# Ones times ones on TensorE: 253 matmuls into unread PSUM banks, in the waits of a decoder step on one Trainium2 core

## The reference

```python
x = x + 0.5 * _swiglu(_rmsnorm(x, lw['g_ffn1']), lw['w1_gate'], lw['w1_up'], lw['w1_down'])
h = _rmsnorm(x, lw['g_mix'])
proj = h @ lw['w_in']
...
y_a = _rmsnorm(attend(q_a, k_a, v_a, logf_a), lw['g_out_a'])
...
h_m, C, n, m = _mlstm(q_m, k_m, v_m, i_pre, log_f_m, C0, n0, m0)
y_m = jax.nn.sigmoid(o_m).reshape(B, T, H_M, HEAD_DIM) * _rmsnorm(h_m, lw['g_out_m']).astype(x.dtype)
y = jnp.concatenate([y_a.reshape(B, T, W_A), y_m.reshape(B, T, W_M)], axis=-1) @ lw['w_out']
x = x + y
x = x + 0.5 * _swiglu(_rmsnorm(x, lw['g_ffn2']), lw['w2_gate'], lw['w2_up'], lw['w2_down'])
```

## Time and profile before

| | |
|---|---|
| median of 3 runs | 2433.18 us (2431.02 to 2445.05) |
| profiled execution | 2432.46 us, span 2430.5 us |
| TensorE matmul busy | 2353.8 us, 97% of the span, 17537 instructions |
| TensorE weight load busy | 2279.3 us, 94% |
| VectorE busy | 1245.9 us, 51% |
| ScalarE busy | 842.9 us, 35% |
| chain that ended last, by engine | TensorE 92%, VectorE 5%, ScalarE 1%, DMA 1% |
| mean granted TensorE clock | 0.979 |

### The profile page before, as it was taken

How to read it: one execution, slowest core, us unless ns; L and a number is a source line. 1 busy time by engine, 2 the same in 40 slices (tenths; PEclk the granted TensorE clock), 3 DMA queues, 4 the chain that set the end, 5 groups by cost and what they waited for, 6 DMA issues and landing times.

```text
span 2430.5 us, 47588 instructions
## 1 busy us (share of the span) xinstructions
PE 2353.8 (97%) x17537; PEld 2279.3 (94%) x17537; DVE 1245.9 (51%) x1848; ACT 842.9 (35%) x1109; POOL 83.6 (3%) x96
## 2 busy tenths in 40 slices
PE   7999999999999999997999898999999999999998
PEld 6999999999999999875999667999999999999998
DVE  6554444454454464563457665464445444455543
ACT  4433333333332443341234232443333233333332
POOL 2000000000000010000001240000000000000000
PEclk9999999999999999987999897999999999999999
DMA  5555555555554444454545332455555445555553
GB/s 159 179 158 170 166 162 173 171 162 168 165 163 167 153 158 148 151 175 152 168 160 172 97 107 70 164 165 167 162 166 162 166 169 167 170 158 167 161 170 127
DMA packets 175660, 383.90 MB, mean 158 GB/s; under 512 B 18949, under 2 KB 44669, under 8 KB 175245
## 3 DMA queue, kind: packets, MB, share of 16 engines
q1 hardware_dynamic: 172736, 375.98, 48.9%
q0 software_dynamic: 2432, 5.57, 0.7%
q10 hardware_dynamic: 416, 1.32, 0.2%
HBM read 373.09 MB, written 9.70 MB: 157 GB/s over the span
## 4 chain that ended last, share of the span: by engine, by line
PE 92%; DVE 5%; ACT 1%; issue 1%; DMA 1%; POOL 0%; SPq 0%; ACTq 0%; DVEq 0%; POOLq 0%
PE ps L1487 29%; PE ps L1489 28%; PE ps L1488 28%; DVE w_lo L882 1%; PE ps L1713 1%; PE ps L1572 1%; PE ps L1890 1%; PE ps L1535 1%; PE ps L1726 0%; PE ps L1881 0%; PE ps L1542 0%; ACT w_hi L568 0%; DMA x_rows<-in_x_sample 0%; DVE xt L908 0%; POOL C L521 0%
## 5 line engine op out<-in xcount | busy, mean ns | idle before, releaser
L882 DVE TENSOR_TENSOR w_lo<-w_raw,w_hi 128x1024 fp32r<-128x1024 f32 (+1 forms) x690 | 788.8, 1185 | 1034.9 <-ACT w_hi L568 1034.3
L568 ACT CAST w_hi<-w_raw 128x1024 fp32r<-128x1024 f32 (+1 forms) x690 | 669.2, 1017 | 1322.1 <-PE ps L1489 1319.3
L1487 PE MATMUL ps<-x_hi,w_hi 128*128 128x288 f32 (+1 forms) x2752 | 815.9, 296 | 5.2 <-DVE w_lo L882 3.2
L1489 PE MATMUL ps<-x_hi,w_lo 128*128 128x288 f32 (+1 forms) x2752 | 813.4, 296 | 0.0
L1488 PE MATMUL ps<-x_lo,w_hi 128*128 128x288 f32 (+1 forms) x2752 | 808.1, 294 | 0.0
L1487 PEld LDWEIGHTS ps<-x_hi,w_hi 128*128 128x128 f32 x2752 | 517.3, 188 | 6.4 <-DVE w_lo L882 3.3
L1488 PEld LDWEIGHTS ps<-x_lo,w_hi 128*128 128x128 f32 x2752 | 521.5, 189 | 0.1
L1489 PEld LDWEIGHTS ps<-x_hi,w_lo 128*128 128x128 f32 x2752 | 517.8, 188 | 0.0
L1487 PE MATMUL ps<-hid_hi,w_hi 128*128 (+1 forms) x1376 | 407.2, 296 | 1.5 <-DVE X L1053 1.5
L1488 PE MATMUL ps<-hid_lo,w_hi 128*128 (+1 forms) x1376 | 406.9, 296 | 0.0
L1489 PE MATMUL ps<-hid_hi,w_lo 128*128 (+1 forms) x1376 | 406.8, 296 | 0.0
(11 more groups left out here) (405 smaller groups left out, 1465.4 us busy)
## 6 DMA issues: line engine op xcount, KB each, us to landing
w_raw<-in_w_down SPq DMA_DIRECT2D x178, 512.0 KB
w_raw<-in_w_gate SPq DMA_DIRECT2D x320, 256.0 KB
w_raw<-in_w_up SPq DMA_DIRECT2D x320, 256.0 KB
w_raw<-in_w_in SPq DMA_DIRECT2D x64, 512.0 KB
w_raw<-in_w_in SPq DMA_DIRECT2D x64, 384.0 KB
w_raw<-in_w_out SPq DMA_DIRECT2D x32, 512.0 KB
page<-in_cache_k SPq DMA_DIRECT2D x16, 512.0 KB, 3.6
w_raw<-in_w_gate SPq DMA_DIRECT2D x32, 192.0 KB
```

Source lines behind the costliest of these rows:

```text
L568: nc.scalar.copy(w_hi[:, slot, 0:width], w_raw[:, slot, 0:width]).then_inc(w_hi_ready, 1)
L882: nc.vector.tensor_tensor(w_lo[:, slot, 0:width], w_raw[:, slot, 0:width], w_hi[:, slot, 0:width].bitcast(F32), ALU.subtract).then_inc(w_l ...
L1487: mm(out, hi, x_hi[:, k, :], start=first and pair == 0 and s == slots[0], stop=False)
L1489: ins = mm(out, lo, x_hi[:, k, :], start=False, stop=last and pair == 1 and s == slots[-1])
```

## The change

A function `keep_busy(bank, n)` issues n float32 matmuls of the 128 x 128 matrix of ones by itself into a bank. They set no semaphore, and nothing reads what they write. It is called at eight places of TensorE's stream: 12 and 32 around the transpose of the gains, 1 in each of the last nine steps of the input's transposes, 24 after the sequences' logits, 2 after each of the 16 pages, 32 after the transposes of the state, 48 after the sequences' scores in the mixer, and 64 after the head sums. That is 12 + 32 + 9 + 24 + 32 + 32 + 48 + 64 = 253 matmuls. Two waits are added: for `ones` (`pool_const` 1) ahead of the first, and for `s_all_ready` ahead of the 48, a wait that stands later in the stream too. The other engines' streams are as before.

```diff
+        def keep_busy(bank, n):
+            for _ in range(n):
+                mm(ps[:, bank, 0:P], ones[:, :], ones[:, :], start=True, stop=True)
...
+        pe.wait_ge(pool_const, 1)
+        keep_busy(7, 12)
         pe.wait_ge(pool_const, 4)
         pe.wait_ge(sem("g1_loaded"), 16)
         tr(ps[:, 0, 0:KD], g1_rows[:, :], ident[0:KD, 0:KD]).then_inc(sem("g1T_done"), 1)
+        keep_busy(7, 32)
         for t in range(KD):
             pe.wait_ge(sem(f"x_loaded{t // 8}"), 48)
             if t >= 7:
                 pe.wait_ge(sem("xT_copied"), t - 6)
+                keep_busy(0, 1)
...
         ins.then_inc(sem("sample_logits"), 1)
+        keep_busy(3, 24)
         for g2 in range(2):
             pe.wait_ge(sem("sample_p"), g2 + 1)
...
             ins.then_inc(sem("sample_pv"), 1)
+            keep_busy(3, 2)
         pe.wait_ge(sem("out_rows_ready"), 1)
...
         ins.then_inc(sem("edges_done"), 1)
+        keep_busy(2, 32)
         pe.wait_ge(sem("ext_edges"), 2)
         pe.wait_ge(sem("ya_ready"), H + 1)
         groups_products(groups["in_m"], 4, xm_hi, xm_lo, (sem("xn_ready"), 16))
...
         ins.then_inc(sem("ws_scores"), 1)
+        pe.wait_ge(sem("s_all_ready"), 2)
+        keep_busy(7, 48)
 
         pe.wait_ge(sem("conv_rows_ready"), 4)
         pe.wait_ge(sem("qn_ready"), 1)
...
         head_sums(SUM_Y, 1, range(H, 2 * H))
+        keep_busy(7, 64)
         head_spread(1, "xn_tmp", 0, 1)
```

## The result

The changed kernel took 2445.21 us, the median of 9 runs, against 2431.02 us before (9 runs): a ratio of 1.0047, 95% interval 1.0027 to 1.0067. It is slower, by some 11 us: less than the 1% at which the prediction drew its line, clear of no change by its interval, and beyond the forecast's range of 2426 to 2442 us. The profiled execution spans 2443.5 us, 13.0 us more than the one before. TensorE's mean granted clock rose, from 0.979 to 0.985, and the time rose with it.

A forecast was written before the change was run, and what follows sets the result against it. TensorE, busy 97% of the span, was taken as the bound. Start -0.4, attention's end +0.7, mixer -2.2 and roots +4.8 gave +2.9 us on 2432.46 us; forecast 2435.5 us, range given 2426 to 2442 us.

The forecast's parts named there:

- The sign: Whole kernel: the change makes it slower, by +2.9 us.
- the mechanism of the bursts: TensorE's stream: a started burst runs out whatever the wait, and the work behind it stands until then.
- the verdict "within 1%": Whole kernel: the time stays within about 1%, 24 us, of no change; chance 0.94.
- The price of a ones matmul: Every burst: n ones take 0.225n us at the full clock or 0.43n us at half.
- The pages: Attention's end: 0.44 us a page plus 0.45 us of ones, hidden by transfers; last page at 1128.9 us; whole term +0.7 us.
- The start: Input's transposes: begin at 13.6 us, steps of 0.5 us at full clock, ones 0.22 us each; -0.4 us.
- The clock after the waits: Behind waits: first products at half clock, the mixer's projections at full, the output projection at half.
- Rival 1: Wherever ones are put: the clock holds, also for first products, first head and output projection; -5.9 us, 2426.6 us; chance 0.13.
- Rival 2: Start: the clock falls under the input's transposes, steps of 0.86 us; +6.2 us there, 2441.7 us in all; chance 0.10.
- The mixer: First head: 48 ones cost +3.5 us, full clock gives 7.4 us back, one clock loss costs 1.7 us; -2.2 us.
- The roots: Ahead of `head_spread`: 64 ones take 14.4 us against a 9.03 us wait, VectorE paces the spread; +4.8 us.

The follow-up runs named there:

- no_pages: Changed kernel without the 32 ones matmuls behind the pages: 2440.06 us, ratio to the kernel before 1.0036 (1.0022 to 1.0049).
- start_short: Kernel before with ones at the start alone, 12 then 14, none between the transposes' steps: 2425.63 us in one run, beside 2431.29 us before.
- after_again: The changed kernel profiled once more, unchanged; no run time given; from L1366 to the second head 40.9 us, where the first profile took 37.1.
- mixer_only: Kernel before with the wait for `s_all_ready` and the 48 ones in the mixer alone: 2432.50 us in one run.
- pages_only: Kernel before with 2 full ones matmuls behind each page alone: 2439.07 us in one run, beside 2430.78 us before.
- pages_narrow: Kernel before with 2 ones matmuls of 32 columns behind each page: 2433.62 us in one run, beside 2430.78 us before.
- fitted_guard2: Kernel before with bursts cut to their waits, 4 ones ahead of the first head and one in each head: 2432.3 us, ratio 0.9991.

## Why the prediction was wrong

The sign, the mechanism of the bursts and the verdict "within 1%" were right. The size was not: +2.9 us were forecast, +13.0 us came in the profiled execution and about +11 us by the ratio of the runs.

- **The price of a ones matmul** was right where ones follow ones: 0.23 us at full (64 records, 32 matmuls, in 7.3 us); at half the first 12 took 5.5 us, 0.46 us each with their start, where 0.43 us was charged. A burst always ran out, as stated.
- **The pages: the step that failed.** "Then each page has its 0.44 us (...) and 0.45 us of ones" came out as 0.57 and 0.64. The 0.44 us is the pace of pages that overlap with each other, and the 0.225 us that of ones behind ones; put in turn, neither pace holds. The row that gives 0.44 us says `128*32`, the ones say `128*128`; I added two paces of streams that cannot be mixed at their paces. 16 times 0.33 us are 5 us, and since "it is used up to the last tenth" no cover was left to hide it. From the logits to L1366 the changed kernel lost 6.4 us (4.6 us in its second profile) where +0.7 was forecast, and no_pages gave back 5.4 us of that; by the ratios of the runs it gave back 2.7 us, with overlapping intervals. This is the largest of the misses, and not the only one.
- **The start** was forecast at -0.4 us and came out at +1.7 us (two stages). The burst ended where I put it (14.1 instead of 13.6 us), but a step is 0.53 instead of 0.50 us, a step's ones 0.29 instead of 0.22 us, and the products behind ran 5.8 us at half, longer than the 5.0 us before. start_short shows what was there to be had: 5.4 us.
- **The clock after the waits** was right at each place: down behind the 3.21 us wait, up at the projections, down again at the output projection. Rival 1 fell with that. Rival 2 fell too: no step of the changed kernel took 0.86 us, and in start_short 48 transposes in a row, without any ones, kept 0.54 us a step. The rule of the Trainium skill's page "TensorE: Matmul & The Clock Gate", Part 4 (PE-mode transpose), that the clock gate does not take transposes for work, is neither borne out whole nor refuted whole. For it: 13.8 us of transposes before did not raise the clock, and in start_short it fell 0.4 us behind the last one. Against it: in after_again the clock rose at 1360.2 us, after 4.2 us in which TensorE did nothing but the mixer's transposes. The prediction took the mixer's transposes for a steady case at full clock; in 9 of 16 profiles they were not.
- **The mixer** was forecast at -2.2 us and came out at -1.3 us, in mixer_only -1.2 us, but at +2.5 us in after_again, outside the ends of -3.9 and +1.5. The fall in the first head lasted twice what I charged (6.8 us), three times in after_again, and a fall under the transposes had no term at all.
- **The roots** were forecast at +4.8 us: +5.1 - 0.6 = +4.5 us here, +5.1 - 0.7 us alone. VectorE paces the spread, as stated.
- **Two slips in the sums.** The upper end of the start, 13.6 + 7 x 0.6 + 9 x 0.85, is 25.5 us and not 26.5, so +1.5 us; and 7.4 us given back in the mixer goes with a stretch of 16.3 us, while the 15.6 us named give 7.1. Neither bears on the miss.
- **Chance.** Seven heads and head sums +3.6 us, attention -2.0 us: together +1.6 us of the 13.0 us are probably not the change's, as far as the repeated kernels tell. The forecast had no term for it, and its range should have had one: before's own two profiles differ by 2.9 us in the seven heads alone. That would not have saved the range, since the ratio over 9 runs gives 11 us too.

## What to carry to other kernels

A warming burst costs its overrun in full wherever TensorE is the bottleneck, so cut it to the shortest wait it fills: by the ratios, the same idea was +11 us with 253 full matmuls and -12 us with 96 full and 32 narrow ones. Put filler only where the work behind it is bound by TensorE (it bought nothing ahead of the spread that VectorE paces), in the shape of its neighbours, and never add the pace of one stream to that of another when their tile shapes differ. And where a clock comes and goes by itself, profile the unchanged kernel twice before giving a difference of 3 us to the code.

## What the runs showed of the hardware

- A matmul over 128 columns between groups over 32 columns costs 0.33 us beside its own 0.22 us (pages_only: 1.22 us a page with two of them, 0.44 us without any); in the neighbours' shape, 0.11 us apiece (pages_narrow: 0.66 us with two).
- Behind a burst, 48 transposes in a row ran at the full clock (start_short: 8.72 us), and it fell 0.4 us behind the last; from half the clock, the same 48 did not raise it (before: 13.80 us). The mixer's 24 transposes ran at full in 7 profiles and in 9 with a fall among them; in after_again the clock rose again while nothing else had run for 4.2 us. What makes the difference is not shown.
- In mixer_only the clock fell in L1888, products on 32 partitions, behind others on 32 and 8 partitions and with no wait on TensorE for 16 us. Four full matmuls ahead of them went with a first head at full clock in both kernels that had them (in fitted_guard2 but for its last 1.3 us); one full matmul in each head went with more falls, not fewer.
